# Splitting expert weights into high and low parts: two pieces of 1024 columns become one of 2048

## What is computed

```python
for gi in range(N_EXPERT_GROUPS):
    sl = slice(gi * EXPERTS_PER_GROUP, (gi + 1) * EXPERTS_PER_GROUP)
    h1 = jnp.einsum('td,edf->tef', x, w1[sl])
    h3 = jnp.einsum('td,edf->tef', x, w3[sl])
    act = jax.nn.silu(h1) * h3 * combine[:, gi, :, None]
    out = out + jnp.einsum('tef,efd->td', act, w2[sl])
```

## Time and profile before

| | us |
|---|---|
| median of three runs | 1691.87 |
| the profiled execution | 1683.87 |
| its span, first to last instruction | 1681.9 |
| the 36 tiles from the start of xcl(3) to the start of xcl(39) | 349.68 |
| of these, VectorE busy | 328.29 |
| TensorE busy (matmul records) | 312.81 |
| ScalarE busy | 299.44 |

### The profile page before, as it was taken

The page is one execution under the profiler, slowest core; times in us unless marked ns, Lnnn a source line. Parts: engine busy times, 40 slices in busy tenths (PEclk is TensorE's granted clock), DMA queues, the critical chain, the costliest instruction groups (busy, mean ns, idle before and its releaser), DMA issues. The chain is left out here.

```text
span 1681.9 us, 26627 instructions
## 1 busy us (share of the span) xinstructions
PE 1403.0 (83%) x8709; PEld 1242.7 (74%) x8709; DVE 1284.3 (76%) x2063; ACT 765.5 (46%) x1189; POOL 335.7 (20%) x382
## 2 busy tenths in 40 slices
PE   2899989899898998989893999997078998998980
PEld 2898887888888898887892899975067777777760
DVE  4148989989898898989987445533469999999974
ACT  3135253343534335243342333312058888888861
POOL 0123322333123233222220000000301111111112
PEclk9599998999989899898996999998579999999995
DMA  4142341714316252252533724403188999998936
GB/s 142 26 120 71 91 132 51 191 44 134 101 41 189 60 156 70 76 148 62 167 82 128 235 64 149 135 26 122 67 327 324 344 334 331 346 337 336 340 129 224
DMA packets 191349, 271.40 MB, mean 161 GB/s; under 512 B 15884, under 2 KB 154358, under 8 KB 174886
## 3 DMA queue, kind: packets, MB, share of 16 engines
q1 hardware_dynamic: 178350, 245.62, 45.1%
q0 software_dynamic: 9968, 18.25, 3.1%
q10 hardware_dynamic: 2992, 7.03, 1.1%
HBM read 237.95 MB, written 50.26 MB: 171 GB/s over the span
## 5 line engine op out<-in xcount | busy, mean ns | idle before, releaser
L759 PE MATMUL pu<-xh,wh 128*128 128x304 f32 (+1 forms) x1280 | 290.1, 310 | 46.0 <-DVE wl L233 39.3
L759 PE MATMUL pu<-xl,wh 128*128 128x304 f32 (+1 forms) x1280 | 281.1, 302 | 0.0
L759 PE MATMUL pu<-xh,wl 128*128 128x304 f32 (+1 forms) x1280 | 279.3, 301 | 0.0
L759 PEld LDWEIGHTS pu<-xh,wh 128*128 128x128 f32 x1280 | 207.6, 200 | 51.9 <-DVE wl L233 41.1
L759 PEld LDWEIGHTS pu<-xl,wh 128*128 128x128 f32 x1280 | 209.6, 200 | 0.0
L759 PEld LDWEIGHTS pu<-xh,wl 128*128 128x128 f32 x1280 | 207.1, 199 | 0.0
L233 POOL TENSOR_TENSOR wl<-ring,wh 128x1024 fp32r<-128x1024 f32 x48 | 119.7, 2494 | 356.3 <-ACT wh L502 354.3
L886 DVE SCALAR_TENSOR_TENSOR cacc<-a_p,gc,cacc 128x528 f32<-128x528 f32 x232 | 189.7, 818 | 0.0
L1998 DVE TENSOR_TENSOR W13l<-W,W13h 128x1024 fp32r<-128x1024 f32 x160 | 184.8, 1216 | 5.0 <-ACT W13h L1950 4.8
L502 ACT ACTIVATE wh<-ring 128x1024 fp32r<-128x1024 f32 x80 | 84.3, 1055 | 192.8 <-PE pu L759 191.4
L1909 PE MATMUL eh<-W13h,xch 128*128 128x512 f32 x320 | 131.0, 409 | 43.4 <-DVE xcl L1998 39.1
(11 more groups left out here) (392 smaller groups left out, 2858.9 us busy)
## 6 DMA issues: line engine op xcount, KB each, us to landing
W<-in_exp_w SPq DMA_DIRECT2D x120, 1024.0 KB, 8.2
ring<-in_w_in SPq DMA_DIRECT2D x80, 512.0 KB, 4.1
stage<-decay_rows SPq DMA_DIRECT2D x8, 1120.0 KB, 7.1
x<-in_state_ssm SPq DMA_DIRECT2D x16, 512.0 KB, 7.0
out_new_ssm_sample<-x SPq DMA_DIRECT2D x16, 512.0 KB, 8.3
wraw<-in_ssm_out_w SPq DMA_DIRECT2D x8, 1024.0 KB, 9.7
Ed<-decay_rows SPq DMA_DIRECT2D x32, 140.0 KB, 7.3
gates<-gbuf ACTq DMA_DIRECT2D x16, 280.0 KB, 2.1
```

Source lines behind the costliest of these rows:

```text
L759: last = pe.matmul(u_cols(r, a, b), w[:, k % RING, j, :], x[:, j, a:b], start=(j == 0 and n == 0), stop=(j == KD - 1 and n == 2))
```

## The change

CH goes from 4 to 2 and CH2 from 2 to 1. W13h and W13l of a tile are written in two pieces of 2048 columns, W2h and W2l in one piece of 2048. The counts on the semaphores follow through `finished`. Loads, matmuls, their order and all other instructions stay.

```diff
-        CH, CH2 = 4, 2
+        CH, CH2 = 2, 1
         KC = KD // CH
...
             def split_down(i, b):
                 act.wait_ge(s_w2[b], loads(i, b))
                 act.wait_ge(s_y, finished(i - 2))
-                for c in range(CH2):
-                    act.activation(W2h[:, b, c, :], W2[:, b, D * c:D * c + D], ACT.Copy).then_inc(s_w2h, 1)
+                act.activation(W2h[:, b].rearrange("p c d -> p (c d)"), W2[:, b], ACT.Copy).then_inc(s_w2h, 1)
...
             def split_down(i, b):
                 dve.wait_ge(s_y, finished(i - 1))
-                for c in range(CH2):
-                    dve.wait_ge(s_w2h, finished(i - 1, CH2) + c + 1)
-                    low(W2l[:, 0, c, :], W2[:, b, D * c:D * c + D], W2h[:, b, c, :]).then_inc(s_w2l, 1)
+                dve.wait_ge(s_w2h, finished(i - 1, CH2) + 1)
+                low(W2l[:, 0].rearrange("p c d -> p (c d)"), W2[:, b],
+                    W2h[:, b].rearrange("p c d -> p (c d)")).then_inc(s_w2l, 1)
```

## The result

| | before | after |
|---|---|---|
| median of nine runs of each, us | 1690.87 | 1699.18 |
| ratio of after to before, 95% interval | | 1.0044 (1.0027 to 1.0061) |
| profiled execution, us | 1683.87 | 1697.97 |
| its span, us | 1681.9 | 1696.0 |

The changed kernel is slower by 0.44%, some 7.4 us by the ratio, 8.3 us by the medians; 8.0 us were forecast.

What follows compares the result with a forecast made beforehand. VectorE's list, 9.71 us per tile, bounds the kernel, nearly equalled by a two-tile chain through ScalarE and TensorE. Chain +5.9, start +2.2 and last tile -0.06 give +8.0 us: 1699.9 us, range 1693 to 1703.5.

Steps and rivals of the forecast that it cites:

- Part 1: VectorE's list in the experts block: merged pairs shorten it by 0.18 us per tile to 9.53, alone 6.5 us faster.
- Part 2: Two-tile chain through ScalarE: W13l waits for 2048 columns of W13h, 2.03 us handoff, 9.88 us per tile, +5.9 us.
- rival 1: Experts block: VectorE's list stays the bound, about -4.7 us, 1687.2 us; chance 8%.
- Rival 4: TensorE's longer gap lowers its clock in the experts block, some 2 us per stretch, above 1703; chance 2%.
- Part 3: W2l waits for all of W2h: free while W13l's wait covers it, otherwise up to 0.3 us every second tile.
- Part 4: Block start, tiles 0 to 3: longer first pieces count in full, 0.75 + 0.75 + 0.67 = +2.2 us.
- Part 5: Weight reloads keep 4 us spare, TensorE waits only through xcl; last tile's W2l saves 0.06 us.

Runs made afterwards that it cites:

- short_first: Changed kernel with W13 in pieces of 1024, 1024 and 2048 columns on both engines, W2 still in one: 1691.01 us, ratio to before 0.9994.
- w13_only: Kernel before with only W13 in two pieces of 2048 columns, W2 staying in two pieces: 1701.62 us, ratio to before 1.0057.
- act4_dve2: Changed kernel, but ScalarE writes W13h in four pieces while VectorE keeps two for W13l; W2 in one: 1701.17 us, ratio to before 1.0059.
- act2_dve4: Changed kernel, but VectorE writes W13l in four pieces while ScalarE keeps two for W13h; W2 in one: 1701.70 us, ratio to before 1.0062.
- early_load_after: Changed kernel with the register loads ahead of xcl and xch issued early, behind the first W13 piece: 1676.73 us, ratio to before 0.9924.
- w2_only: Kernel before with only W2 in one piece of 2048 columns, W13 staying in four: 1688.20 us, ratio to before 0.9997.

## Why the prediction was right, and where it was off

**VectorE's list (Part 1).** The shortening is there: the W13l of a tile take 4.49 us instead of 4.62, W2l 2.28 instead of 2.35, together 0.20 us per tile where 0.18 was forecast, and a pair occupies 4.49 - 2.29 = 2.20 us where 2.21 was named. (In the even tiles the gap ahead of xcl grew from 0.55 to 0.68 us, which takes 0.13 us back there; no wait is listed for it, and the reason is open. Busy time fell by only 3.5 us in 36 tiles, in part because a W13l that waits no longer overlaps the end of al.) It brought nothing, as forecast. The Trainium skill's rule on grouping (Perfetto Trace Analysis, section "Optimizing Scalar/DVE Operations") did not decide here although VectorE was busy 94% of the time: busy time fell and the time rose. Its sentence on bubbles fits, as short_first shows: it cuts one piece and has the time of before again (0.9994).

**The chain (Part 2).** The mechanism is the one forecast: distance fixed, VectorE idle ahead of W13l, 0.24 us where 0.3 was named, TensorE waiting longer for xcl. One reading was wrong: ScalarE does not go from thh to W13h "without a gap". It stands 0.33 us ahead of xch, with its register load:

```profile
1357.84 1.07 ACT L1962 ACTIVATE xch<-xc 128x1024 fp32r x1 [0.33 <-issue]
```

So ScalarE did have something to gain, which the forecast denied when it weighed rival 1; with the early loads W13h starts 4.21 us behind thh and not 4.65. It did not change the outcome, since this kernel leaves that gap where it is. Two sizes were off, in opposite directions. The handoff was put at 2.03 us and is 1.95, the lower bound from the earlier trace rows: ScalarE's 1.92 us and 0.03 us for the signal, not 0.1. So a tile takes 9.85 us where 9.88 was forecast, and the 34 tiles from xcl(5) on cost 4.6 us more than before, not 5.6. Against this, xcl(3) to xcl(5) took 21.27 us instead of 19.45, 1.8 us more, of which 0.3 were forecast.

**Rival 4 in small.** Most of those 1.8 us are the clock, in tile 3 alone. TensorE's first up matmul of tile 3 and the window around it (columns as above):

```profile
1281.76 0.62 PE L1909 MATMUL eh<-W13h,xch 128*128 128x512 f32 x1 [1.30 <-DVE xcl L1997]
```

```profile
1280.00:1289.00 9.00, 7.70 (x27) 6.12 (x28) 8.16 (x5) 5.23 (x5) 2.44 (x1) 0.81 0.92 328
```

The granted clock is 0.81 over these 9 us, so part of it lay at 1.2 GHz; up to then TensorE had waited 0.36 us for `ac`, done two transposes and waited 1.30 us for xcl. thh(3) comes 8.83 us behind xcl(3), not 7.26: 1.6 us. The same stands in w13_only and act4_dve2 (8.86 and 8.81 us), but not in act2_dve4 and early_load_after (7.25 and 7.23), whose W13l of tile 3 waits just as long. In act2_dve4 TensorE waited no less, 0.51 us for `ac` and 1.30 us for xcl, and the clock stayed at 1.00:

```profile
1283.74 0.49 PE L1910 MATMUL eh<-W13h,xch 128*128 128x512 f32 x1 [1.30 <-DVE xcl L1998]
```

Nor does the lateness decide: behind the cast, xcl(3) comes at 64.20 us in w13_only and at 64.32 us in act2_dve4. What decides it is open. Behind tile 3 the clock is 1.00 up to xcl(39), as forecast.

**W2 (Part 3).** The W2h that follows thh(11) is that of tile 11, not 12; the times read are right. For the change itself the step held: in the changed kernel W2l stands 2.00 us behind W2h, a wait, in every second tile from tile 23 on (2.04 to 2.18 us in the odd tiles 5 to 21), by which it starts up to 0.2 us late, and the wait at W13l covers it. What the forecast missed is that this wait closes a chain of its own, 9.73 us per tile in w2_only. It was called free as long as covered, with up to 0.3 us in every second tile if not; the third chain is that price, some 0.15 us in two tiles, and by the trace it is why w2_only did not gain its 2.2 us.

**The start (Part 4).** W13l of tiles 0, 1 and 3 stands 2.01, 2.02 and 2.01 us behind its W13h, where 1.16 us were seen before and 2.03 forecast. The handoffs are right, but the sum, +2.4 us against +2.2, is right in part by luck. W13h of tile 0 starts 16.04 us behind the cast, not 15.37, which is 0.67 us that arose ahead of the first changed instruction; in the experiments this distance is 15.66 to 16.14 us, with pieces of either length. Behind it W13l of tile 0 ends another 0.7 us later and that of tile 1 another 0.8, where 0.75 was forecast for each. From xcl(1) to xcl(3) only 0.2 us were added where 0.67 was forecast, because 11 up matmuls of tile 1 ran at the lower clock and not 13: thh(1) comes 9.43 us behind xcl(1), not 9.84, which gives back 0.4 us. The prediction had named that case and taken no change.

**What does not move (Part 5), and the sum.** From tile 3 on no wait of ScalarE for a load of weights is listed; the end is 0.5 us shorter, and as it differs by up to 2 us between the experiments nothing follows from that. The sum, +8.0 against +8.4 in the two traces, owes its closeness in part to errors that offset each other: about 1.0 us too much for the handoff and 1.5 us too little for the clock in tile 3, and in the start the 0.7 us that the change did not make against the 0.4 us that the clock gave back.

## What to carry to other kernels

Even when an engine is busy 94% of the time, walk the closed chains through the other engines: one with less slack than a change adds to its handoff takes over, and fewer, longer instructions then lose time. The first piece of a split sets how soon the next engine may start, so a producer's first piece should stay short where the consumer's wait for it lies on the chain that sets the pace, whatever is done with the rest. A consumer that starts, tile after tile, the same short time after the end of a producer's piece (0.03 and 0.10 us here) is waiting for it, even where no idle time is listed; a steady distance alone does not show that, as the 1.58 us in w2_only do.

## What the hardware showed that was not expected

The signal from ScalarE to VectorE had two lengths on the same line. In tiles 0, 1 and 3 VectorE starts about 0.1 us behind the end of W13h (1.16 us for 1.055 before, 2.01 us for 1.91 after), and in the tiles from 5 on 0.03 us (1.95 for 1.92); the same 0.07 us lies between 2.11 and 2.04 us in act4_dve2. The instructions of tiles 0, 1 and 3 stand outside the loop, those from tile 4 on inside it, but the vh and vl of the block `mixer`, outside any loop, have 0.03 us as well, and W2l, where it waits inside the loop, starts 0.10 us behind the end of W2h (2.00 us for 1.90 in w2_only). So the loop alone does not decide it, and no run here shows the reason.

The register load shows 0.55 us of idle time on VectorE. Moving it took 5.96 - 5.33 = 0.63 us from the distance between W13l and xcl, because xcl then also overlaps the tail of `ac` (by 1403.03 + 0.42 - 1403.37 = 0.08 us).
